# Products of 64x64 blocks in a chunked delta-rule mixer: taken with 128 stationary columns and all 128 rows

## What is computed

```python
A = eye + jnp.where(strict, kk, 0.0)                 # lower triangular
T = lax.linalg.triangular_solve(A, eye, left_side=True, lower=True, unit_diagonal=True)
u = jnp.einsum('bnhij,bnjhd->bnhid', T, v_beta)
w = jnp.einsum('bnhij,bnjhd->bnhid', T, k_beta * jnp.exp(gc)[..., None])
# then a scan over the chunks: v_new = u - w S; o = q S e^g + (q k) v_new; S = S e^g + k_dec v_new
```

## Time and profile before

| | us |
|---|---|
| median of 3 runs | 2515.11 |
| lowest, highest | 2512.35, 2515.34 |
| the profiled execution | 2516.23 |
| its span | 2514.3 |
| TensorE busy | 2457.1 (98%) |
| TensorE weight loads busy | 2248.9 |
| VectorE busy | 1398.6 (56%) |
| ScalarE busy | 695.7 (28%) |
| GpSimd busy | 221.5 (9%) |

### The profile page before, as it was taken

The page is one execution under the profiler, slowest core; times in us unless marked ns, Lnnn a source line. Parts: engine busy times, 40 slices in busy tenths (PEclk is TensorE's granted clock), DMA queues, the critical chain, the costliest instruction groups (busy, mean ns, idle before and its releaser), DMA issues.

```text
span 2514.3 us, 36115 instructions
## 1 busy us (share of the span) xinstructions
PE 2457.1 (98%) x13660; PEld 2248.9 (89%) x13660; DVE 1398.6 (56%) x2481; ACT 695.7 (28%) x1425; POOL 221.5 (9%) x370
## 2 busy tenths in 40 slices
PE   6999999999999999999999999999999999999997
PEld 5999999999888887799899998988888989989986
DVE  6445654596766665654554445446645445454555
ACT  5323331211544443312121121213311211212213
POOL 4000011000323333200000000000100000000002
PEclk9999999999799999999999999999999999999999
DMA  5123344322754453511111111212411211111101
GB/s 160 44 70 107 102 120 116 127 76 107 234 151 147 146 147 110 205 44 58 34 53 47 50 50 33 67 34 67 152 50 34 66 34 48 52 33 50 50 25 76
DMA packets 219420, 212.23 MB, mean 84 GB/s; under 512 B 32284, under 2 KB 190336, under 8 KB 215980
## 3 DMA queue, kind: packets, MB, share of 16 engines
q1 hardware_dynamic: 219316, 210.84, 26.8%
HBM read 161.11 MB, written 49.79 MB: 84 GB/s over the span
## 4 chain that ended last, share of the span: by engine, by line
PE 56%; DVE 1%; POOL 1%; issue 0%; ACT 0%; DMA 0%; DVEq 0%; POOLq 0%; ACTq 0%
PE bank L122 18%; PE bank L124 18%; PE bank L123 18%; PE bank L2217 1%; PE bank L2215 1%; PE bank L2261 1%; POOL ff_rs L101 0%; DVE f_h_lo L2109 0%; DVE f_acc L2052 0%; DVE xn L2098 0%; ACT f_relu L140 0%; DVE f_acc L152 0%; POOL ff_rt L109 0%; DMA xn<-x_dram 0%; POOL ff_rs L111 0%
## 5 line engine op out<-in xcount | busy, mean ns | idle before, releaser
L2052 DVE TENSOR_TENSOR f_acc<-bank,f_acc 128x512 f32<-128x512 f32 x512 | 351.2, 691 | 296.3 <-PE bank L124 296.0
L122 PE MATMUL bank<-f_h_hi,f_up_lo 128*128 128x344 f32 (+1 forms) x1536 | 490.8, 320 | 0.7 <-issue 0.6
L124 PE MATMUL bank<-f_h_hi,f_up_hi 128*128 128x344 f32 (+1 forms) x1536 | 489.8, 319 | 0.0
L123 PE MATMUL bank<-f_h_lo,f_up_hi 128*128 128x344 f32 (+1 forms) x1536 | 489.5, 319 | 0.0
L122 PE MATMUL bank<-f_dn_hi,f_z 128*128 128x512 f32 x1024 | 399.2, 390 | 0.5 <-DVE x_s L2052 0.5
L124 PE MATMUL bank<-f_dn_hi,f_z 128*128 128x512 f32 x1024 | 398.8, 389 | 0.0
L123 PE MATMUL bank<-f_dn_lo,f_z 128*128 128x512 f32 x1024 | 398.8, 389 | 0.0
L122 PE MATMUL bank<-h_hi,w_lo 128*128 128x412 f32 (+1 forms) x960 | 337.1, 351 | 0.0
L123 PE MATMUL bank<-h_lo,w_hi 128*128 128x412 f32 (+1 forms) x960 | 336.1, 350 | 0.0
L124 PE MATMUL bank<-h_hi,w_hi 128*128 128x412 f32 (+1 forms) x960 | 335.9, 350 | 0.0
L2067 DVE TENSOR_TENSOR f_sqr<-f_relu 128x344 f32<-128x344 f32 (+1 forms) x192 | 99.0, 516 | 359.8 <-ACT f_relu L1984 358.4
(11 more groups left out here) (381 smaller groups left out, 2934.9 us busy)
## 6 DMA issues: line engine op xcount, KB each, us to landing
up_raw<-in_w_up_dram SPq DMA_DIRECT2D x64, 512.0 KB, 4.7
f_dn_raw<-in_w_down_dram SPq DMA_DIRECT2D x64, 512.0 KB, 3.4
p_dram<-ffn_gains SPq DMA_DIRECT2D x24, 1024.0 KB, 4.6
up_raw<-in_w_in_dram SPq DMA_DIRECT2D x24, 512.0 KB, 5.5
up_raw<-p_dram SPq DMA_DIRECT2D x48, 256.0 KB, 5.3
xn<-p_dram SPq DMA_DIRECT2D x32, 256.0 KB, 5.2
xres<-in_x_prompt_dram SPq DMA_DIRECT2D x16, 512.0 KB, 5.3
x_dram<-x SPq DMA_DIRECT2D x16, 512.0 KB, 3.1
```

The costliest lines, as they stand in the source:

```text
L122: pe.matmul(out, wl, xh, start=start and k == 0, stop=False, skip_group_check=skip)
L123: pe.matmul(out, wh, xl, start=False, stop=False, skip_group_check=skip)
L124: last = pe.matmul(out, wh, xh, start=False, stop=stop and k == n - 1, skip_group_check=skip)
L2052: dve.tensor_tensor(dst, bank, dst, ALU.add).then_inc(s["y_added"], 1)
```

## The change

For x and y each matmul takes 128 stationary columns: its own head's block of 64 and a neighbour's beside it (`pair`; for the first three heads the one behind, for the last head the one ahead), and all 128 rows, with zeros against the half that must not count. The rows of `N21` below partition 64 are zeroed once by GpSimd, `xs` gets 128 partitions and is zeroed once by VectorE. The result of heads 0 to 2 lies in the low 64 partitions of bY, that of head 3 in the upper 64, so each copy out of bY is in two instructions.

```diff
-    xs = sb("xs", [HALF, H * HALF])
+    xs = sb("xs", [P, H * HALF])
...
+    def pair(tile, h):
+
+        at = min(h, H - 2) * HALF
+        return tile[:, at:at + P]
...
             pe.wait_ge(s["u_turned"], f + 1)
+            if f == 0:
+                pe.wait_ge(s["n21_zeroed"], 1)
             for h in range(H):
-                last = pe.matmul(head(bY[0:HALF, :], h, HALF), head(N21[f % 2][HALF:P, :], h, HALF), head(U, h)[HALF:P, HALF:P],
+                last = pe.matmul(head(bY, h, HALF), pair(N21[f % 2], h), head(U, h)[:, HALF:P],
                                  start=True, stop=True)
...
             for h in range(H):
-                last = pe.matmul(head(bY[0:HALF, :], h, HALF), head(T64[f % 2][0:HALF, :], h, HALF), head(xs[:, :], h, HALF),
+                last = pe.matmul(head(bY, h, HALF), pair(T64[f % 2], h), head(xs, h, HALF),
                                  start=True, stop=True)
...
             dve.wait_ge(s["y_ready"], f + 1)
-            dve.tensor_copy(heads(U[0:HALF, :])[:, :, HALF:P], heads(bY[0:HALF, 0:H * HALF])).then_inc(s["u_final"], 1)
+            blocks = heads(U[0:HALF, :])[:, :, HALF:P]
+            dve.tensor_copy(blocks[:, 0:H - 1, :], heads(bY[:, 0:H * HALF])[0:HALF, 0:H - 1, :])
+            dve.tensor_copy(blocks[:, H - 1, :], head(bY, H - 1, HALF)[HALF:P, :]).then_inc(s["u_final"], 1)
...
             act.wait_ge(s["x_ready"], f + 1)
-            act.activation(xs[:], bY[0:HALF, 0:H * HALF], ACT.Copy).then_inc(s["xs_made"], 1)
+            if f == 0:
+                act.wait_ge(s["xs_zeroed"], 1)
+            act.activation(xs[0:HALF, 0:(H - 1) * HALF], bY[0:HALF, 0:(H - 1) * HALF], ACT.Copy)
+            act.activation(head(xs, H - 1, HALF)[0:HALF, :], head(bY, H - 1, HALF)[HALF:P, :], ACT.Copy).then_inc(s["xs_made"], 1)
...
             dve.memset(ms[:], 1.0).then_inc(s["zeroed"], 1)
+            dve.memset(xs[:], 0.0).then_inc(s["xs_zeroed"], 1)
...
             pool.wait_ge(c.tb_stored, 32)
+            pool.memset(N21_room[0:HALF, :], 0.0).then_inc(s["n21_zeroed"], 1)
```

More of the change, by code:

```diff
@@ L1205, in mix @@
     names = """kt_loaded qt_loaded0 qt_loaded1 v_loaded gate_loaded vb_loaded ut_loaded gb_loaded t64_loaded0 t64_loaded1 n21_loaded0 n21_loaded1 xres_loaded0 xres_loaded1
-        x1_stored0 x1_stored1 delta_stored         zeroed
+        x1_stored0 x1_stored1 delta_stored zeroed n21_zeroed xs_zeroed
         pt_v pt_g pt_b pt_q pt_k qk_ready x_ready y_ready p_ready gm_ready w_ready o_ready sd_ready oT_ready wo_ready
```

## The result

The changed kernel took 2519.37 us in the median of 14 runs (2515.95 to 2521.55), the kernel before 2514.07 us in 14 runs (2510.39 to 2520.26; the three of the table above are among them). The ratio is 1.0017 with a 95% interval of 1.0010 to 1.0024: 4.3 us slower (2.5 to 6.0). The forecast was +2.6 us, at 2517.7 us.

What follows compares the result with a forecast made beforehand. TensorE, busy 98% of the span, was taken as the bound; 2.2 us there plus 0.4 on VectorE in early passes gave +2.6 us, 2515.1 + 2.6 = 2517.7 us, range 2514 to 2524.

Steps and rivals of the forecast that it cites:

- The price of a group: TensorE, x and y groups: last matmul ahead to second projection matmul takes 1.24 us against 1.15, +0.09 and +0.08.
- The steady passes: TensorE pays 0.17 us in full in each pass from 3 to 15: 13 x 0.17 = 2.2 us.
- the prediction's other estimate: Trainium skill's weight load of columns / 1.2 GHz, 0.107 us for 128: 0.10 us a pass, forecast about 1 us lower.
- VectorE's second copy: Splitting VectorE's y copy adds 0.13 us a pass (0.06 to 0.2), hidden when steady, paid in passes 0 to 2: 0.4 us.
- The room: Steady passes: VectorE's residual add ends at 802.33, TensorE needs it at 802.93, so 0.6 us of added VectorE time fits.
- The gaps stay: Rival, slower: gaps at both borders of 26 groups remain, +0.32 us a group, +8.7 in all, 2523.8 us; 8%.
- VectorE becomes late: Rival, slower: small copy stretched by 0.84 us, TensorE stalls 0.1 to 0.2 us in 13 passes, +2 more, 2520 us; 4%.
- The clock gains: Rival, lower: fuller y of pass 15 prevents the half clock at 974.7, 1.5 us back, +1.1, 2516.2 us; 12%.
- a half-clock stretch that was not there: Sign of a wrong forecast: the changed kernel's trace shows half clock where the trace before had none; no size given.

Runs made afterwards that it cites:

- two heads a product: Changed kernel with two products a group instead of four, each holding two heads' results, no zero padding for them; ratio 1.0011 against the kernel before, median 2517.49 us.
- the move: Second half of VectorE's residual add put ahead of mask product and copies: ratio 0.9996 on the kernel before; with two heads in each product 0.9976, 2509.36 us.

## Why the prediction was right, and where it was off

**The price of a group: right to 0.01 us.** 1.24 us for both, from a row with the same stationary shape and one with 8 moving columns. The moving width did not matter, as argued. Row by row the first distance inside the group is 0.058 and the step out 0.084 us, against 0.112 and 0.031 with 128 moving columns, but the sum is the same.

**The steady passes: right in mechanism, 0.4 us small.** 2.2 us were forecast for the 13 passes from 3 to 15, 0.17 each. Twelve of them lie in the middle part and cost 0.20 each, which makes 2.6 for thirteen. The distance inside a group is 0.112 us, as the row of U by R had it, and not the 0.107 of the prediction's other estimate. The groups give 0.18 of a period's 0.20 us. The other 0.02 to 0.03 us lie between the matmuls of the projection, and no run tells what they are.

**VectorE's second copy: the step that was mis-sized.** Forecast 0.13 us, with 0.06 to 0.2 as bounds; measured 0.28. The bounds came from instructions that all begin to read at the same partition. For a copy of that kind 0.06 was right. It still cost nothing in the steady passes, as forecast. The room was 0.41 us, not 0.6. In the early passes the forecast had 0.4 us. Pass 2 paid 0.11 to 0.13, near the 0.13 forecast although the copy was twice as dear. For passes 0 and 1 the measured size would give up to 0.56, which no total resolves, since the first part scatters from 682.8 to 689.1 us among the traces of the five runs that differ from the kernel before only by a copy, by zeroed rows or not at all.

**The gaps stay: the rival fell, and its price was low.** The gaps went with the narrow shape, as rows of U by R had said. Where they do stay with 128 columns, in the run with 64 rows, a group costs 0.42 us more than before and not 0.32: eight steps grow by 0.053 and not six, since the first distance and the step out, which I had counted with the gaps and taken as fixed, grow with the columns too.

**VectorE becomes late: fell in this kernel, true in another.** The small copy wasn't stretched. But the same wait for the residual add appeared at once when TensorE became faster, and decided between two heads a product with and without the move.

**The clock gains: the stretch went, but not shown to be for the fuller y.** The stretch just behind y of pass 15 is there in both traces of the kernel before (974.7, 974.4) and in neither of the changed kernel, whose last part is 1.8 to 1.9 us shorter. But three other kernels lack it too: the one with head 3's copy from the upper half and the kernel before with the add moved, both with y as before, and the one with 128 rows and 64 columns. So it can go without the fuller y, and why it goes stays open. The stretches at 670.6 and 997.2 came in one trace each of the changed kernel. They are the prediction's sign of being wrong, "a half-clock stretch that was not there"; since two traces of one kernel differ in such stretches, that sign says little.

**The total.** The intervals of both comparisons, 2.5 to 6.0 us and 0.3 to 4.8, hold 2.6 and also the 3.3 that the measured sizes would give (2.6 + 0.11 + 0.56). Both ratios are within the 0.2% that was called no change, and both intervals lie above 1. That the total came out so near has luck in it: two terms were forecast too small, and in both pairs of traces a shorter last part set off a longer first and middle part.

## What to carry to other kernels

Filling a small product up to the full array trades longer weight loads for the gaps at the borders of a narrow group: here 0.37 us for 0.29, a small loss, because each group had eight matmuls between two borders; an estimate from the same numbers is that up to six it would be a gain (5 x 0.053 is under 0.29), which wasn't tried. Zero padding in only one dimension gets nothing or worse, and columns that are paid for should hold work that counts: two heads in a product gained 0.36 us a group over the narrow blocks. Ask of a saving on the bound engine who is late next: here one move on VectorE turned +0.1% into -0.24%.

## What the runs showed of the hardware

Neighbouring copies out of a bank overlap by 0.07 to 0.08 us on VectorE when both read the low 64 partitions, and not at all when the second reads the upper 64: 0.39 against 0.61 us for the pair, and 0.21 against 0.35 us from one start to the next on ScalarE. All copies here write the low 64 partitions, so the part of the writing side is not shown. The residual add behind the pair, over all 128 partitions, overlaps the copy from the low half too (by 0.07 us) and not the one from the upper half.

The gaps at the borders of a group that does not use the full array are there for 128 rows by 64 columns as much as for 64 by 128 and 64 by 64, about 0.3 us for the two together.

Half clock lengthens what it falls in: in thirteen traces the part from x of pass 15 on took 1545.2 to 1546.7 us with 6.8 us of it ahead of the stretch at the very end, and 1550.8 to 1551.4 us with 20.4. Two executions of one program differ in where such stretches fall, by as much as this change is worth.
